# A two-layer hybrid block: mixer with 512-column projection groups, split block weights and key/value units in halves

## The reference

```python
proj = u @ w_in                                    # 1024 -> 2032 columns
p_mla, p_nsa, p_fox, p_s5 = jnp.split(proj, [MLA_IN, MLA_IN + NSA_IN, MLA_IN + NSA_IN + FOX_IN], axis=-1)
# MLA: c_q 192, c_kv 128, k_pe 32; normed, projected up, causal attention, 4 heads
# NSA: q 256, six keys/values of 64, gates 12; attention over compressed, selected and windowed keys
#   compress: 15 blocks of 32 tokens x 64 -> gelu(blocks @ phi_w1[j] + b1) @ phi_w2[j], phi_w1[j] is 2048 x 256, j = 0, 1
# FOX: q, k, v of 256, 4 forget logits, causal attention with cumulative log-forget
# S5: 16 complex diagonal state groups over 256 columns, gelu, gated
y = _rmsnorm(jnp.stack([o_mla, o_nsa, o_fox, o_s5], axis=2), group_g).reshape(B, S, MIX_WIDTH)
return y @ w_out
# cross attention: kv = mem_n @ w_kv (1024 -> 2048)
```

## Time and profile before

| | |
|---|---|
| median of 3 runs | 1339.74 us (1339.5 to 1340.98) |
| profiled execution | 1336.82 us, span 1335.0 us, mean granted clock 0.991 |
| busy: TensorE, its weight loads | 1300.9 us, 1125.5 us |
| busy: DVE, ACT, GpSimd | 823.0 us, 665.3 us, 239.6 us |
| HBM read | 221.84 MB, 168 GB/s over the span |

### The profile page before, as it was taken

One profiled execution on the slowest core, in us unless ns is written; L12 is line 12 of the kernel. 1 busy time (PEld: TensorE's weight loads), 2 busy tenths in 40 slices (PEclk: granted clock), 3 DMA queues, 4 the chain that ended last, 5 costly groups with the idle time before them and its releaser, 6 DMA issues.

```text
span 1335.0 us, 19566 instructions
## 1 busy us (share of the span) xinstructions
PE 1300.9 (97%) x7348; PEld 1125.5 (84%) x7348; DVE 823.0 (62%) x1141; ACT 665.3 (50%) x1085; POOL 239.6 (18%) x250
## 2 busy tenths in 40 slices
PE   7999999999999999999999999999999999999998
PEld 5887888989998978888878878899899888788886
DVE  5657856765546656555576587567655665755554
ACT  6455445463336454444364555454544454644443
POOL 1728902000002010000036197010000020100000
PEclk9999999999979999999999999999999999999999
DMA  9654644225323436555555545542353343555551
GB/s 342 247 189 157 212 166 174 95 95 193 126 92 127 155 130 258 184 187 185 187 199 190 184 171 185 184 150 94 118 214 105 113 175 113 221 189 189 189 189 63
DMA packets 32734, 224.81 MB, mean 168 GB/s; under 512 B 3616, under 2 KB 4128, under 8 KB 6816
## 3 DMA queue, kind: packets, MB, share of 16 engines
q1 hardware_dynamic: 30368, 211.37, 44.5%
q10 hardware_dynamic: 2304, 12.58, 2.5%
HBM read 221.84 MB, written 2.10 MB: 168 GB/s over the span
## 4 chain that ended last, share of the span: by engine, by line
PE 90%; issue 3%; ACT 2%; DVE 2%; POOL 1%; DMA 1%; SPq 0%; ACTq 0%; DVEq 0%; POOLq 0%
PE PS L1676 86%; PE PS L1802 1%; DVE w_lo L1139 1%; DMA raw<-in_weights 1%; PE PS L1969 1%; POOL st L515 1%; ACT work L959 0%; ACT x_hi L707 0%; ACT w_hi L666 0%; DVE h L1142 0%; PE PS L2073 0%; PE PS L1751 0%; PE PS L1896 0%; PE PS L2202 0%; PE PS L1954 0%
## 5 line engine op out<-in xcount | busy, mean ns | idle before, releaser
L1139 DVE TENSOR_TENSOR w_lo<-raw,w_hi 128x1024 fp32r<-128x1024 f32 (+3 forms) x382 | 484.3, 1312 | 216.7 <-ACT w_hi L666 213.4
L666 ACT ACTIVATE w_hi<-raw 128x1024 fp32r<-128x1024 f32 (+2 forms) x372 | 369.3, 1043 | 219.8 <-PE PS L1676 200.1
L1676 PE MATMUL PS<-w_hi,x_hi 128*128 128x512 f32 (+4 forms) x1248 | 457.2, 366 | 9.3 <-DVE w_lo L1139 5.6
L1676 PE MATMUL PS<-w_lo,x_hi 128*128 128x512 f32 (+4 forms) x1248 | 446.7, 358 | 0.0
L1676 PE MATMUL PS<-w_hi,x_lo 128*128 128x512 f32 (+4 forms) x1248 | 439.4, 358 | 0.0
L1676 PEld LDWEIGHTS PS<-w_hi,x_hi 128*128 128x128 f32 x1248 | 238.4, 191 | 46.9 <-DVE w_lo L1139 6.9
L1676 PEld LDWEIGHTS PS<-w_hi,x_lo 128*128 128x128 f32 x1248 | 237.8, 191 | 35.0
L1676 PEld LDWEIGHTS PS<-w_lo,x_hi 128*128 128x128 f32 x1248 | 238.6, 191 | 32.4 <-issue 0.5
L515 POOL TENSOR_SCALAR st<-st 128x1 f32<-128x1 f32 x32 | 25.5, 796 | 633.3 <-ACT proj L689 571.2
L1676 PE MATMUL PS<-w_hi,hid_hi 128*128 128x512 f32 x320 | 124.9, 390 | 0.0
L1676 PE MATMUL PS<-w_lo,hid_hi 128*128 128x512 f32 x320 | 124.5, 389 | 0.0
(11 more groups left out here) (271 smaller groups left out, 1375.3 us busy)
## 6 DMA issues: line engine op xcount, KB each, us to landing
raw<-in_weights SPq DMA_DIRECT2D x196, 1024.0 KB, 4.8
pmat<-in_mats ACTq DMA_DIRECT2D x3, 1664.0 KB, 7.8
gain<-in_post ACTq DMA_DIRECT2D x8, 512.0 KB, 3.7
zone<-mem_scratch ACTq DMA_DIRECT2D x2, 1024.0 KB, 4.8
raw<-in_weights SPq DMA_DIRECT2D x3, 512.0 KB, 7.6
h<-in_x SPq DMA_DIRECT2D x2, 512.0 KB, 6.3
zone<-in_mem SPq DMA_DIRECT2D x1, 1024.0 KB, 10.9
mem_scratch<-zone ACTq DMA_DIRECT2D x1, 1024.0 KB, 10.6
```

The source lines that it names most:

```text
L666: a.activation(o[:, c_], i[:, c_], ACT.Copy).then_inc(sem[hi_done[s]], 1)
L1139: return v.tensor_tensor(o, x_, y_, op)
L1676: return t_.matmul(o, a_, b_, start=first, stop=last)
```

## The change

- The input projection is eight units in four groups (`IN_GROUPS`). Group 0 is two units: the compressed, selected keys and values (256 columns by tokens, `first_rows_half`) and S5 by features. Groups 1 to 3 are 496, 512 and 512 columns wide, each of two units that hold four k-tiles each; a group is done for one token half, then for the other (`group`, `group_half`), into a whole bank.
- At the mixer's start rows are transposed and filled by token half (`rows_of`, `fill_hi_of`, `post_norm_and_fill`).
- The `phi_w1` units are split like all others. The blocks are split too (in the idle FFN tiles `hid_hi`, `hid_lo`), high and low part side by side as 30 stationary columns: per k-tile one matmul of `w_hi` against 30 columns and one of `w_lo` against 15, each 256 columns wide. A fold matrix in the constants adds the two row sets.
- A key/value unit is done in halves (`kv_half`), which stand between attention steps; the second of these units comes ahead of phi. There are 32 units in the mixer now, so slots shift from layer to layer.
- S5's output tiles are split into `hid_hi`, `hid_lo`; group outputs are transposed into banks 6, 4 and 7, and the values of attention 2 follow the first half of the first output unit.
- On ACT and DVE the order of evacuations, splits, MLA, S5 and NSA steps follows TensorE's.

The core of the diff (constants, offsets, unchanged patterns and renumbered units are cut):

```diff
-IN_UNITS = [[(I_S5, I_END)], [(I_CQ, I_CKV)], [(I_CKV, I_NQ)], [(I_NQ, I_KC)], [(I_KC, I_KW)],
-            [(I_KW, I_FQ), (I_FF, I_S5)], [(I_FQ, I_FK)], [(I_FK, I_FV)], [(I_FV, I_FF)]]
+IN_GROUPS = [[(I_KC, I_KW)], [(I_CQ, I_NQ), (I_KW, I_FQ), (I_FF, I_S5)], [(I_NQ, I_KC), (I_FQ, I_FK)],
+             [(I_FK, I_FV), (I_FV, I_FF)]]
```

On ACT:

```diff
                 split_mid(0)
                 split_mid(1)
                 y_squares(0)
+                fill_hi_of(1, 0, range(6))
                 h_square(1, 0)
-                fill_hi(1)
+                fill_hi_of(1, 0, (6, 7))
+                fill_hi_of(1, 1, range(6))
+                evac(0, 0)
+                fill_hi_of(1, 1, (6, 7))
...
+                split_mid(4)
+                evac(0, 1)
                 split_mid(3)
...
+                evac(1, 0)
+                split_mid(5)
+                evac(1, 1)
...
+                split_mid(9)
...
+                evac(3, 1)
+                act.wait_ge(*E.at("mem_in", 16))
+                for k in range(KT):
+                    a.activation(xh3[:, k], zone[:, 2048 + k * S:2048 + (k + 1) * S], ACT.Copy,
+                                     scale=pcol[:, C_MEM + k:C_MEM + k + 1]).then_inc(sem["x_hi_done"], 1)
                 attention(0)
...
+                split_mid(10)
+                act.wait_ge(*E.at("blocks_done", 1))
+                for j in range(2):
+                    i = a.activation(blocks[j][:, :, 0:NC_CMP], bl[:, j], ACT.Copy)
+                i.then_inc(sem["blocks_hi"], 1)
+                evac_kv(0)
                 attention_t(0)
+                split_mid(11)
+                split_mid(13)
+                evac_kv(1)
...
+                split_mid(12)
                 split_mid(14)
+                attention(3)
```

On DVE:

```diff
-                post_norm(0, 0.5)
-                fill_lo(1)
                 split_mid(1)
+                post_norm_and_fill(0, 0.5, E.at, 1)
+                fill_lo_of(E.at, 1, 1, range(KT))
...
+                split_mid(5)
                 tt(s_tmp[0], s_tmp[0], s_tmp[1], ALU.add)
                 E.step(tt(s_tmp[2], s_tmp[2], s_tmp[3], ALU.subtract))
...
+                mem_lo(range(2))
                 attention_max(0)
+                mem_lo(range(2, KT))
+                split_mid(9)
...
+                split_mid(10)
...
+                dve.wait_ge(*E.at("blocks_hi", 1))
+                for j in range(2):
+                    i = tt(blocks[j][:, :, NC_CMP:2 * NC_CMP], bl[:, j], blocks[j][:, :, 0:NC_CMP].bitcast(F32), ALU.subtract)
+                i.then_inc(sem["blocks_done"], 1)
+                attention_copy(0)
```

On TensorE:

```diff
-                rows_transposed(1)
+                def first_rows_half(t, ks):
...
+                    for k in ks:
+                        pe.wait_ge(*E.at("x_split", FILL[FI_MIX] + KT * t + k + 1))
+                        i = three([(x_tile(k, t), (w_hi[s][:, k * UC:(k + 1) * UC], w_lo[s][:, k * UC:(k + 1) * UC]))],
+                                  bank((4, 1)[t])[:, 0:UC], k == 0, k == KT - 1)
+                    return i
+                def group_half(g, t, half):
+                    s, _, ns = mid(l, 2 * g + half)
+                    w = sum(b - a_ for a_, b in IN_GROUPS[g])
+                    if half == 0 and 2 * g + t > 2:
+                        pe.wait_ge(*E.at("proj_done", 2 * g + t))
+                    pe.wait_ge(*E.at(split_done[s], ns + 1))
+                    for k in range(KT // 2):
+                        c_ = slice(k * 2 * UC, k * 2 * UC + w)
+                        i = three([(x_tile(half * KT // 2 + k, t), (w_hi[s][:, c_], w_lo[s][:, c_]))], bank(t)[:, 0:w],
+                                  half == 0 and k == 0, half == 1 and k == KT // 2 - 1)
+                    if t == 1:
+                        i.then_inc(sem[unit_done[s]], 1)
+                    elif half == 1:
+                        i.then_inc(sem["proj_half"], 1)
...
+                keep_clock(7, 2)
+                rows_of(1, 0, range(6))
+                first_rows_half(0, range(KT // 2))
+                rows_of(1, 0, (6, 7))
+                first_rows_half(0, range(KT // 2, KT)).then_inc(sem["proj_half"], 1)
+                rows_of(1, 1, range(6))
...
+                first_rows_half(1, range(KT)).then_inc(sem[unit_done[s]], 1)
...
+                group(1, 0)
...
                 i.then_inc(sem["s5_v"], 1)
+                group(1, 1)
+                group(2, 0)
...
                 i.then_inc(sem["mla_t1"], 1)
-                token_unit(4)
+                group(2, 1)
...
                 i.then_inc(sem["mla_qkv"], 1)
-                token_unit(5)
+                group_half(3, 0, 0)
...
                 i.then_inc(sem["s5_y"], 1)
-                token_unit(6)
+                group_half(3, 0, 1)
...
                 i.then_inc(sem["mla_t2"], 1)
-                token_unit(7)
+                group(3, 1)
                 scores(0)
...
                 i.then_inc(sem["s5_z"], 1)
-                token_unit(8)
+                kv_half(0, 0)
...
                 i.then_inc(sem["nsa_t"], 1)
-                kv_unit(9)
+                kv_half(0, 1)
                 probs_transposed(0)
-                phi_unit(10)
+                pe.wait_ge(*E.at("xkv_done", 1))
+                kv_half(1, 0)
                 times_values(0)
+                phi_unit(M_PHI)
...
                 i.then_inc(sem["fox_cum"], 1)
-                phi_unit(11)
+                kv_half(1, 1)
...
                 fox_heads(I_FK, 2, "fox_tk")
+                phi_unit(M_PHI + 1)
...
                 i.then_inc(sem["s5_rstd_all"], 1)
-                phi_unit(12)
                 scores(3)
-                phi_unit(13)
-                kv_unit(14)
+                pe.wait_ge(*E.at("s5_out", 1))
+                kv_half(2, 0)
+                phi_unit(M_PHI + 2)
+                kv_half(2, 1)
                 probs_transposed(3)
-                kv_unit(15)
+                phi_unit(M_PHI + 3)
+                kv_half(3, 0)
                 times_values(3)
...
                 i.then_inc(sem["phi_t"], 1)
+                kv_half(3, 1)
...
                 i.then_inc(sem["phi_out"], 1)
...
+                def phi_unit(m):
...
+                    for k in range(KT):
+                        b_ = blocks[j][:, half * KT + k]
+                        wh, wl = (w[s][:, k * UC:(k + 1) * UC] for w in (w_hi, w_lo))
+                        first, last = half == 0 and k == 0, half == 1 and k == KT - 1
+                        if first:
+                            mm(o[0:2 * NC_CMP], b_, wh, True, False)
+                        mm(o[0:NC_CMP], b_[:, 0:NC_CMP], wl, False, False)
+                        if not first:
+                            i = mm(o[0:2 * NC_CMP], b_, wh, False, last)
+                def kv_half(q, part):
+                    s, n, ns = mid(l, KV_UNITS[q])
+                    pe.wait_ge(*E.at(split_done[s], ns + 1))
+                    for k in range(KT):
+                        if q == 0 and part == 0:
+                            pe.wait_ge(*E.at("x_split", FILL[FI_MEM] + k + 1))
+                        if q < 4:
+                            c_ = slice(k * UC + part * P, k * UC + (part + 1) * P)
+                            i = three([((w_hi[s][:, c_], w_lo[s][:, c_]), (xh3[:, k], xl3[:, k]))],
+                                      o[:, part * S:(part + 1) * S], k == 0, k == KT - 1)
...
```

More of the change, by code:

```diff
@@ L1103, in _ @@
                 xa_hi(2)
-                split_mid(32)
+                split_mid(M_O + 3)
                 xa_out(3)
                 xa_hi(3)
-                split(*ffn_unit(1, "first"))
-                split(*ffn_unit(1, "second"))
+                split(*ffn_unit(l, 1, "first"))
+                split(*ffn_unit(l, 1, "second"))
                 y_squares(2)
@@ new lines, in _ @@
+                for j in range(2):
+                    for k in range(KT):
+                        if j == 0:
+                            if k == KT // 2:
+                                rows_of(1, 1, (6, 7))
+                            pe.wait_ge(*E.at("x_split", FILL[FI_MIX] + KT + k + 1))
+                        i = three([((w_hi[s][:, k * UC + j * P:k * UC + (j + 1) * P],
+                                     w_lo[s][:, k * UC + j * P:k * UC + (j + 1) * P]), (xh3[:, k], xl3[:, k]))],
+                                  bank(5)[:, j * S:(j + 1) * S], k == 0, k == KT - 1)
@@ L2125, in _ @@
                 i.then_inc(sem["cmp_s"], 1)
[L2127 removed]
+                kv_half(4, 1)
+                kv_half(5, 0)
                 pe.wait_ge(s_con, 16)
@@ L2141, in _ @@
                 i.then_inc(sem["cmp_t"], 1)
-                kv_unit(19)
+                pe.wait_ge(*E.at("xkv_done", 5))
+                kv_half(6, 0)
+                kv_half(6, 1)
                 pe.wait_ge(*E.at("att_out", 3))
@@ L2151, in _ @@
                 i.then_inc(sem["cmp_o"], 1)
-                kv_unit(20)
+                pe.wait_ge(*E.at("xkv_done", 6))
+                kv_half(7, 0)
```

(1 more changed line is left out.)

637 lines of the change are left out of this document (307 added, 330 removed).

## The result

The changed kernel takes 1330.57 us (median of nine runs, 1324.71 to 1331.65). The kernel before took 1336.55 in its nine runs, 3.2 less than the median of three that the prediction started from. The ratio is 0.9938, with a 95% interval of 0.9921 to 0.9955: faster by 0.6%, 6 to 11 us. The profiled execution took 1331.46 us, the one before 1336.82. The forecast of 1330 was met in the sum, but not in its parts: two errors of opposite sign cancelled, and these are the lesson of this case.

What follows compares the result with a forecast made beforehand. TensorE's queue was taken as the bound. Terms of -7.2, -6.8, -0.3, -3.1 and +12.3 gave -5.1 us a layer, the walk -4.2; -4.8 was taken, -9.6 for two, so 1330 us, range 1308 to 1343.

Steps and rivals of the forecast that it cites:

- Input projection: Mixer's input projection: one 256-column unit and 144 wide matmuls, 38.6 us instead of 45.8, -7.2 us a layer.
- the wide matmuls bring nothing: Rival without its own chance: 512 columns cost twice the 0.121 in the input projection, 4 us lost, 1334.
- Phi: Four block-weight units: 1.9 us each instead of 3.59, -6.8 us a layer, bounds 0 and -7.2.
- A: TensorE's wait for `mla_xn` after group(2,0): 2.1 us a layer, about 3.1 by the GpSimd exclusion rule.
- B: TensorE's wait in `kv_half(0,0)` for memory tiles filled behind ACT's and DVE's queues: 3.7 us a layer.
- C: TensorE's wait at `kv_half(1,0)` for `xkv_done`, behind ACT's work after the NSA transposes: 1.9 us a layer.
- D: Wait at `times_values(0)`: DVE's copy stands behind split 10, the S5 gate and the blocks' remainder, 0.9 us a layer.
- E: TensorE's wait at `kv_half(2,0)` for split 14, which DVE ends late: 2.8 us a layer.
- I count the loss as equal: Clock in the rewritten stage: some light spells go, new waits come, layer 0's 9.3 us loss taken as unchanged.
- the clock takes more: Rival, chance 0.14: idle at B and E lowers the clock in both layers; 1339, or 1349 with 40 us more.
- The covers hold: Rival, chance 0.20: two thirds of new waits gone, removals count, -17.4 us a layer; 1305 to 1315, say 1308.
- Splits become the bound: Rival, chance 0.06: the four phi splits lie on the path in full, 19 us more, 1349.

Runs made afterwards that it cites:

- e6: Changed kernel with the first token tile of groups 1 and 2 computed 256 columns at a time: 1330.79 us, ratio 0.9936.
- e3: Changed kernel with MLA's variance ahead of both scans on VectorE and its normalization between them: 1324.27 us, ratio 0.9896.
- e1: Changed kernel with 8, 12 and 12 throwaway matmuls ahead of three TensorE waits of each layer: 1331.51 us, ratio 0.995.
- e5: Changed kernel with 5, 7 and 7 throwaway matmuls ahead of three TensorE waits of each layer: 1325.3 us, ratio 0.99.
- e2: Changed kernel with `phi_unit(M_PHI + 2)` ahead of `kv_half(2,0)` on TensorE: 1321.87 us, ratio 0.9876.
- e4: Changed kernel with all eight memory tiles ahead of `attention_max(0)` on VectorE: 1334.93 us, ratio 0.998.
- e12: e10 with the Ln of the Fox gate and its table load behind `attention_t(0)` on ScalarE: 1311.45 us, ratio 0.9802.
- e9: Changed kernel with phi's packing undone, three matmuls of 15 columns in place of two of 15 and 30: 1336.82 us, ratio 1.0.
- e8: Changed kernel with the first six key/value units computed whole, both halves where the first half stood: 1349.26 us, ratio 1.0081.
- e7: Changed kernel with e2, e3, NSA transposes and 5 throwaway matmuls inside `kv_half(0,0)`'s wait, `evac_kv(0)` and `attention_copy(0)` earlier: 1311.08 us, ratio 0.9791.
- e10: e7 without its five throwaway matmuls in the wait of `kv_half(0,0)`: 1311.35 us, ratio 0.9822.

## Why the prediction was right, point by point

**Input projection, -7.2.** Measured -6.3: the groups after the first take 5.73, 5.45, 5.46, 5.5 (at full clock), 5.98 and 5.56 us, 33.7 in sum against 32.8, mostly since group 3 is in halves around the S5 output. 0.228 for 512 columns held to 0.001. The rival "the wide matmuls bring nothing" is out: 24 of them take 5.45 us, where two of 256 columns in place of each, in e6, take 5.76, only 0.012 more for each pair.

**Phi, -6.8.** 7.6 us (units of 1.9) in place of 14.4: right. The bound of 0.228 was far off; a stationary tile of 30 or 15 columns paces as the 128-column one does.

**The start, -0.3.** Right: from the FFN's end to S5's end 14.07 us, predicted 14.0. The wait in the second half of group 1 is 0.27, predicted 0.6.

**The waits.** A 2.4 (2.1), B 3.0 (3.7), C 0.8 (1.9), D 0.9 (0.9), E 3.0 (2.8): 10.1 against 11.4. All five were where the walk of the three queues put them. C was mis-sized: I counted 1.8 us of ScalarE's exponent-to-tanh work behind the NSA transposes, but it had run beside them. Removed: 1.5 + 1.4 = 2.9 (3.1).
The terms as measured are -6.3 - 6.8 - 0.3 - 2.9 + 10.4 = -5.9 a layer. The stages show -6.3 to -7.3 at full clock; the rest, 0.4 to 1.4, I did not find. The prediction called itself wrong if layer 1 at full clock was not 202 to 204 us. It is 200.3 to 201.3, so by that sign the work was priced wrongly: the waits 1.9 us too high, more than half of it at C, the projection 0.9 too low, and I took -4.8 where my own sum gave -5.1.

The rule of the Trainium skill ("SBUF — State Buffer", "SBUF: two separate sides") would have made A 3.1. The trace has 2.4. Timeline of GpSimd and of VectorE there, in layer 1 of the changed kernel.
```profile
902.02 1.29 POOL L510 TENSOR_TENSOR st<-st,con 128x4 f32<-128x4 f32 x1 [30.25 <-DVE st L1168]
```
```profile
901.75 1.29 DVE L1141 TENSOR_TENSOR work<-work,zone 128x512 f32<-128x512 f32 x2
903.07 0.69 DVE L1141 TENSOR_TENSOR zone<-work 128x512 f32<-128x512 f32 x1
903.80 0.98 DVE L1141 TENSOR_TENSOR proj<-proj,st 128x384 f32<-128x384 f32 x2
```
GpSimd's rstd took 1.29 us here and 1.76 in e3, against 1.01 for the same four columns at 1027.29 us of this trace, so the rows agree with the rule in kind. It cost A nothing: the rstd ended at 903.31, before VectorE was through with its three multiplies at 903.76.

**The clock, "I count the loss as equal".** This is the step that failed. The loss doubled, from 20.5 to 41.0 us at half clock: the rival "the clock takes more" had its mechanism, the new idle stretches in both layers, and its arithmetic, 9.3 us for layer 1. I gave it 0.14 although five new waits of 11 us stood in my own sum. That the total came to 1330 all the same is luck. It didn't reach 1339 because the work came out 1.5 to 2.5 us a layer shorter than forecast, and because the kernel before is 3 us faster over nine runs than over three. e1 and e5 show by fill, and e2 and e3 by order, that the waits cause most of it. The clocks of all executions agree: the mean granted clock is 0.983 in seven of the nine of the changed kernel (0.986 and 0.990 in the others), and 0.985 to 0.993 in the twenty of the kernel before that ran beside e1 to e4.

"HAM oscillation" in "TensorE: Matmul & The Clock Gate" of the Trainium skill names idle gaps as the cause. The runs agree for A, B and E. But the first layer of e12 fell where no wait stands, behind and within stretches of small matmuls, and so did two of the four spells of layer 0 before the change.

**The rivals.** "The covers hold" is out: all five waits came. "Splits become the bound" is out in that form: e9 shows that TensorE's own work still counts nearly in full. Which part pays most is known only for edits alone: the halves 19 us (e8), the packing of phi's two parts 6 to 8 us (e9). No run put the old narrow units or the unsplit phi back alone, or the start by token halves: their gains are read from the rows.

## What to carry to other kernels

Price a wait twice where an engine's clock follows its work: 1.9 us of waiting removed at A gave 3.5, and of the 9.0 us that e2 took off its two stages more than half came through the clock. When a sum of new waits is in the forecast, its clock price belongs into the same sum.

Before calling work "absorbed" by a wait, ask who starts the chain that ends the wait. If it is the same engine, only what lies between the start and the wait can be absorbed (read from e9's rows).

The order of single instructions in three in-order queues was worth more (20 us by the ratio in e7, 16 in e10, which has no throwaway work) than the rewriting of the stage (8 us). Throwaway work in a wait is the worse cure: where it is longer than the wait it costs what the clock gives (e1), and e10 reached e7's median without it.

When an experiment changes nothing, look whether two effects cancelled: e6 lost 1.5 us in layer 1, most of it to a longer wait, and got it back from the clock.
